# The second block's first norm by tokens: squares on ScalarE, the rows turned earlier, the memory's keys turned inside the queries' strip

## The reference

```python
def rmsnorm_2(x, g):
    xf = x.astype(jnp.float32)
    y = xf * lax.rsqrt(jnp.mean(xf * xf, axis=-1, keepdims=True) + EPS)
    return (y * g.astype(jnp.float32)).astype(x.dtype)

h = rmsnorm_2(x, mix_norm[l])
z = h @ w_in[l]            # pool inputs, queries, keys, values, index queries qi, index key ki, weights wi
...                        # heads normed and rotated, index scores, top 64 keys per query, attention
x = x + jnp.concatenate([y_pool, y_attn], axis=-1) @ w_out[l]
...                        # cross attention to 256 memory tokens, with its own normed keys
...                        # mixture of 32 experts, two per token
```

## Time and profile before

| | |
|---|---|
| median of 3 runs | 822.93 us (822.11 to 824.31) |
| the profiled execution | 823.26 us |
| its span in the profile | 821.5 us |
| mean granted TensorE clock | 0.93 of 2.4 GHz |
| TensorE busy | 735.7 us, 90% of the span |
| VectorE busy | 389.3 us, 47% |
| ScalarE busy | 321.0 us, 39% |
| DMA, mean | 257 GB/s |

### The profile page before, as it was taken

How to read it: one execution, slowest core, us unless ns; L and a number is a source line. 1 busy time by engine, 2 the same in 40 slices (tenths; PEclk the granted TensorE clock), 3 DMA queues, 4 the chain that set the end, 5 groups by cost and what they waited for, 6 DMA issues and landing times.

```text
span 821.5 us, 13037 instructions
## 1 busy us (share of the span) xinstructions
PE 735.7 (90%) x5447; PEld 589.6 (72%) x5448; DVE 389.3 (47%) x761; ACT 321.0 (39%) x596; POOL 21.4 (3%) x54
## 2 busy tenths in 40 slices
PE   6699999999999999999998998686889999879785
PEld 4276687897999999999897776675674666545342
DVE  1446996537554555555627798465341111111011
ACT  2335564626444444445544655555340111011011
POOL 4000001000000002000000000000000000000000
PEclk8699998979999999999977999797789999998899
DMA  9998984419667664337341332085777999999996
GB/s 326 398 410 328 410 322 115 154 53 333 231 206 237 213 209 163 128 132 253 118 154 65 117 139 103 11 356 195 266 295 286 420 420 420 421 419 421 421 415 211
DMA packets 71475, 211.44 MB, mean 257 GB/s; under 512 B 7351, under 2 KB 34133, under 8 KB 55542
## 3 DMA queue, kind: packets, MB, share of 16 engines
q1 hardware_dynamic: 70370, 209.91, 67.2%
q0 software_dynamic: 800, 0.63, 0.6%
q10 hardware_dynamic: 244, 0.03, 0.0%
HBM read 209.51 MB, written 1.05 MB: 256 GB/s over the span
## 4 chain that ended last, share of the span: by engine, by line
PE 66%; DMA 10%; DVE 8%; ACT 5%; SPq 5%; issue 4%; ACTq 0%; DVEq 0%
PE ps L1848 10%; PE ps L1849 9%; PE ps L1850 9%; SPq L403 5%; PE ps L1858 5%; PE ps L1859 5%; PE ps L1860 5%; PE ps L2448 4%; DMA ring<-in_expert_w_up_dram 3%; DMA ring<-in_expert_w_gate_dram 3%; PE ps L1909 3%; DMA ring<-in_ada_w_dram 2%; PE ps L1923 2%; DVE LO L1113 2%; PE ps L2424 2%
## 5 line engine op out<-in xcount | busy, mean ns | idle before, releaser
L1113 DVE TENSOR_TENSOR LO<-ring,HI 128x1024 fp32r<-128x1024 f32 (+1 forms) x135 | 163.7, 1221 | 131.2 <-ACT HI L631 131.2
L631 ACT ACTIVATE HI<-ring 128x1024 fp32r<-128x1024 f32 (+1 forms) x135 | 141.2, 1054 | 136.6 <-PE ps L1850 67.4
L1848 PE MATMUL ps<-AH,HI 128*128 128x256 f32 x320 | 91.0, 284 | 0.1
L1849 PE MATMUL ps<-AL,HI 128*128 128x256 f32 x320 | 90.5, 283 | 0.0
L1850 PE MATMUL ps<-AH,LO 128*128 128x256 f32 x320 | 90.5, 283 | 0.0
L2448 PE MATMUL ps<-ring,ZM 128*32 128x256 f32 x880 | 66.6, 401 | 14.1 <-DMA ring<-in_expert_w_up_dram 11.2
L1848 PE MATMUL ps<-HI,AH 128*128 128x512 f32 (+1 forms) x176 | 69.9, 397 | 7.2 <-DVE AL L1131 6.2
L1849 PE MATMUL ps<-LO,AH 128*128 128x512 f32 (+1 forms) x176 | 68.3, 388 | 0.0
L1850 PE MATMUL ps<-HI,AL 128*128 128x512 f32 (+1 forms) x176 | 68.2, 387 | 0.0
L2448 PEld LDWEIGHTS ps<-ring,ZM 128*32 128x32 f32 x880 | 37.0, 115 | 36.8 <-DMA ring<-in_expert_w_up_dram 15.0
L1848 PEld LDWEIGHTS ps<-AH,HI 128*128 128x128 f32 x320 | 61.4, 192 | 2.8 <-issue 2.5
(11 more groups left out here) (374 smaller groups left out, 1288.9 us busy)
## 6 DMA issues: line engine op xcount, KB each, us to landing
ring<-in_expert_w_gate_dram SPq DMA_DIRECT2D x29, 1024.0 KB, 26.0
ring<-in_expert_w_up_dram SPq DMA_DIRECT2D x26, 1024.0 KB, 23.1
ring<-in_ada_w_dram SPq DMA_DIRECT2D x24, 1024.0 KB, 12.7
ring<-in_expert_w_down_dram SPq DMA_DIRECT2D x23, 1024.0 KB, 25.1
ring<-in_w_ffn_in_dram SPq DMA_DIRECT2D x20, 1024.0 KB, 6.4
ring<-in_w_in_dram SPq DMA_DIRECT2D x17, 1024.0 KB, 5.9
ring<-in_w_ffn_out_dram SPq DMA_DIRECT2D x11, 1024.0 KB, 7.2
ring<-in_w_out_dram SPq DMA_DIRECT2D x8, 1024.0 KB, 7.2
```

The source lines that it names most:

```text
L631: act(HI[:, i % UNITS, 0:w], W.view(name)[:, o:o + w], ACT.Copy).then_inc(s_hi, 1)
L1113: tt(LO[:, i % UNITS, 0:w], W.view(name)[:, o:o + w], HI[:, i % UNITS, 0:w].bitcast(F32), ALU.subtract).then_inc(s_lo, 1)
L1848: mm(dst, lh, rh, start=start, stop=False)
L1849: mm(dst, lh, rl, start=False, stop=False)
```

## The change

The norm's sum of squares is no longer made from XC by TensorE. TensorE turns XC into rows by tokens right behind the strip `qi`, into banks 4 to 7, ahead of `kw`. VectorE makes all four copies to X. ScalarE squares the four half rows with sums, and `mean_rs(0)`, `root_rs(0)`, `recip_rs(0)` give `rs`; the two later norms become the second and third of these helpers' rounds, and the counts of `s_sq` and `s_rs` move with them. The eight squares SQ2 on ScalarE and the matmuls over them are gone. `kw` moves to banks 1 and 3 and waits until ScalarE has read the memory's keys there. The memory's keys are turned behind the third of the queries' four units, and the copies to KM move behind: on ScalarE behind Z of `kw` and one more high half, on VectorE behind the sums of the rotated index queries. ScalarE and VectorE split the units of `q` at new places in their lists. No DMA is added, removed or moved. On GpSimd only a count changes: it waits for 12 and not 8 of `s_sq`, which is the same event.

The diff, without constants, counts of semaphores of the later norms and one view:

```diff
 WOB = (0, 1, 4, 5)
-XTB = (4, 1, 3, 5)
+XTB = (4, 5, 6, 7)
 SCB = ((4, 5), (6, 7))
...
 
-                src = X2[:, t, :].rearrange("q (k p) -> q k p", k=8)[:, :, 64 * n:64 * n + 64] if c else X[:, t, 512 * n:512 * n + 512]
+                src = X2[:, t, :].rearrange("q (k p) -> q k p", k=8)[:, :, 64 * n:64 * n + 64] if c == 8 else X[:, t, 512 * n:512 * n + 512]
                 summed(src, ss[:, t, n:n + 1], s_sq, c + i + 1)
 
             def root_rs(i):
-                ac.wait_ge(s_rs, 4 * i + 3)
+                ac.wait_ge(s_rs, 4 * i + 2)
                 act(rs[:, :], rs[:, :], ACT.Sqrt).then_inc(s_rs, 1)
...
                     bias=colm[:, 3, k:k + 1]).then_inc(s_ah, 1)
-                ac.wait_ge(s_xf, k + 1)
-                act(SQ2[:, k, :], XC[:, k, :], ACT.Square).then_inc(s_sqs, 1)
                 if k in (3, 5):
...
                 act(KS[:, t, :], ps[(1, 3)[t]][:, :], ACT.Copy).then_inc(s_ks, 1)
+            hi_to(S.first["q0"])
+            hi_to(S.first["q0"] + 1)
             ac.wait_ge(s_kn, 1)
             act(mst[:, 8:16], mst[:, 8:16], ACT.Sqrt).then_inc(s_kn, 1)
+
+            for i in range(4):
+                ac.wait_ge(s_xt, i + 1)
+                squares(0, i, i // 2, i % 2)
+            root_rs(0)
 
...
 
-            for i in range(4):
-                hi_to(S.first["qi0"] + i + 3)
-            rooted(rs[:, :], ps[5][:, 0:2], SUM_MIX)
-            ac.wait_ge(s_rs, 1)
+            hi_to(S.first["q0"] + 2)
+            ac.wait_ge(s_rs, 4)
             z_out("qi1", 2048, 512, (0, 2), "qi")
-            hi_to(S.first["kw"] + 3)
             for t in range(NT):
                 if t == 0:
                     ac.wait_ge(s_t0, T0["kw"])
                 else:
                     ac.wait_ge(s_un, S.end["kw"])
-                act(Z[:, t, 2560:NZ], ps[6 + t][:, 0:NZ - 2560], ACT.Copy, scale=rs[:, t:t + 1]).then_inc(s_z, 1)
-
-            for i in (1, 3):
-                ac.wait_ge(s_xp, 4 + i + 1)
-                act(X[:, i // 2, 512 * (i % 2):512 * (i % 2) + 512], ps[XTB[i]][:, :], ACT.Copy).then_inc(s_xt, 1)
-            ac.wait_ge(s_hdp, 1)
-            act(KM[:, 0:2, :], ps[6][:, :].rearrange("p (h n) -> p h n", h=2), ACT.Copy, scale=C1[:, XQK + 1:XQK + 2]).then_inc(s_hda, 1)
+                act(Z[:, t, 2560:NZ], ps[(1, 3)[t]][:, 0:NZ - 2560], ACT.Copy, scale=rs[:, t:t + 1]).then_inc(s_z, 1)
+            hi_to(S.first["q0"] + 3)
 
...
 
-            hi_to(S.first["q0"] + 3)
+            ac.wait_ge(s_hdp, 1)
+            act(KM[:, 0:2, :], ps[6][:, :].rearrange("p (h n) -> p h n", h=2), ACT.Copy, scale=C1[:, XQK + 1:XQK + 2]).then_inc(s_hda, 1)
             hi_to(S.first["q0"] + 4)
...
                 tt(rs[:, :], ss[:, :, 0], ss[:, :, 1], ALU.add).then_inc(s_rs, 1)
-                ve.wait_ge(s_rs, 4 * i + 2)
+                ve.wait_ge(s_rs, 4 * i + 1)
                 ts(rs[:, :], rs[:, :], 1.0 / D, EPS, ALU.mult, ALU.add).then_inc(s_rs, 1)
 
             def recip_rs(i):
-                ve.wait_ge(s_rs, 4 * i + 4)
+                ve.wait_ge(s_rs, 4 * i + 3)
                 ve.reciprocal(rs[:, :], rs[:, :]).then_inc(s_rs, 1)
...
 
+            for i in range(4):
+                ve.wait_ge(s_xp, 4 + i + 1)
+                copy(X[:, i // 2, 512 * (i % 2):512 * (i % 2) + 512], ps[XTB[i]][:, :]).then_inc(s_xt, 1)
+
             ve.wait_ge(s_ks, 10)
             ts(mst[:, 8:16], mst[:, 8:16], 1.0 / P, EPS, ALU.mult, ALU.add).then_inc(s_kn, 1)
-            for i in range(4):
-                lo_to(S.first["qi0"] + i + 3)
+            lo_to(S.first["q0"])
+            lo_to(S.first["q0"] + 1)
             ve.wait_ge(s_kn, 2)
             ve.reciprocal(mst[:, 8:16], mst[:, 8:16]).then_inc(s_kn, 1)
-            ve.wait_ge(s_rn, SUM_MIX)
-            ve.reciprocal(rs[:, :], rs[:, :]).then_inc(s_rs, 1)
-            lo_to(S.first["kw"] + 3)
+            mean_rs(0)
             ve.wait_ge(s_kn, 3)
             for t in range(NT):
                 k3 = KS[:, t, :].rearrange("p (h d) -> p h d", h=4)
                 tt(k3, k3, bc(mst[:, 8 + 4 * t:12 + 4 * t], 2, [P, 4, P]), ALU.mult).then_inc(s_kn, 1)
-
-            for i in (0, 2):
-                ve.wait_ge(s_xp, 4 + i + 1)
-                copy(X[:, i // 2, 512 * (i % 2):512 * (i % 2) + 512], ps[XTB[i]][:, :]).then_inc(s_xt, 1)
-            ve.wait_ge(s_hdp, 2)
-            ts(KM[:, 2:4, :], ps[7][:, :].rearrange("p (h n) -> p h n", h=2), C1[:, XQK + 1:XQK + 2], None, ALU.mult).then_inc(s_hdv, 1)
+            recip_rs(0)
+            lo_to(S.first["q0"] + 2)
 
...
             head_sum(2048, 8, 4, s_hqi)
+            ve.wait_ge(s_hdp, 2)
+            ts(KM[:, 2:4, :], ps[7][:, :].rearrange("p (h n) -> p h n", h=2), C1[:, XQK + 1:XQK + 2], None, ALU.mult).then_inc(s_hdv, 1)
             lo_to(S.first["q0"] + 5)
...
             strip(("qi0", "qi1"), (0, 2), OP_MIX, 0, per=2)
-            u, w72 = S.first["kw"], NZ - 2560
-            te.wait_ge(s_lo, u + 1)
-            for t in range(NT):
-                for k in range(8):
-                    hi, lo = parts(u, slice(w72 * k, w72 * k + w72))
-                    ins = exact(ps[6 + t][:, 0:w72], AH[:, k, P * t:P * t + P], AL[:, k, P * t:P * t + P], hi, lo, k == 0, k == 7)
-                ins.then_inc(s_t0 if t == 0 else s_un, 1)
-            for k in range(8):
-                te.wait_ge(s_sqs, SQ_M + k + 1)
-                added_up(5, SQ2[:, k, :], k, 8)
-            te.wait_ge(s_ks, 10)
             for i in range(4):
-                if i == 3:
-                    te.wait_ge(s_rn, SUM_MIX)
                 for k in range(4 * (i % 2), 4 * (i % 2) + 4):
                     ins = tr(ps[XTB[i]][:, P * (k % 4):P * (k % 4) + P], XC[:, k, P * (i // 2):P * (i // 2) + P], ident[:, :])
                 ins.then_inc(s_xp, 1)
-            te.wait_ge(s_z, 4)
+            u, w72 = S.first["kw"], NZ - 2560
+            te.wait_ge(s_lo, u + 1)
+            te.wait_ge(s_ks, 10)
+            for t in range(NT):
+                for k in range(8):
+                    hi, lo = parts(u, slice(w72 * k, w72 * k + w72))
+                    ins = exact(ps[(1, 3)[t]][:, 0:w72], AH[:, k, P * t:P * t + P], AL[:, k, P * t:P * t + P], hi, lo, k == 0, k == 7)
+                ins.then_inc(s_t0 if t == 0 else s_un, 1)
 
...
 
-            te.wait_ge(s_kn, 5)
+            def between_queries(i):
+
+                if i == 2:
+                    te.wait_ge(s_kn, 5)
+                    heads_turned(KS, (6, 7))
+
             te.wait_ge(s_xt, 4)
-            heads_turned(KS, (6, 7))
-            strip(("q0", "q1"), (4, 5), OP_MIX, 0, per=2)
-            te.wait_ge(s_z, 2)
+            strip(("q0", "q1"), (4, 5), OP_MIX, 0, None, between_queries, per=2)
+            te.wait_ge(s_z, 4)
             strip(("k0", "k1"), (0, 1), OP_MIX, 0, per=2)
```

More of the change, by code:

```diff
@@ L120 @@
 RT_AS, RT_NEG = 13, 16
-SQ_X, SQ_A, SQ_G, SQ_B, SQ_U, SQ_F, SQ_M = 0, 4, 6, 8, 10, 18, 26
+SQ_X, SQ_A, SQ_G, SQ_B, SQ_U, SQ_F = 0, 4, 6, 8, 10, 18
 RB_X, RB_A, RB_B, RB_FF, RB_F = 1, 2, 3, 4, 5
-SUM_X, SUM_A, SUM_G, SUM_B, SUM_FF, SUM_F, SUM_MIX = 1, 2, 3, 4, 5, 6, 7
+SUM_X, SUM_A, SUM_G, SUM_B, SUM_FF, SUM_F = 1, 2, 3, 4, 5, 6
 B0, N1, BU, BV, BG, NM, CB, XQK = 0, 16, 24, 28, 32, 36, 44, 48
@@ L222, in build @@
         SQY, GQ = tiles(Zf[:, 0:1024], 4), tiles(Zf[:, 1024:2048], 4)
-        SQ2 = tiles(Zf[:, 3072:5120], 8)
         CV, SG = YT[:, 0:4, :], YT[:, 4:8, :]
@@ L602, in _ @@
                                      bc(hn[:, i, hi:hi + 32], 1, [P, NT, 32]), ALU.mult).then_inc(s_tab, 1)
-            po.wait_ge(s_sq, 8)
+            po.wait_ge(s_sq, 12)
             po.memset(Lp[:, :, 0:4], FILL).then_inc(s_set, 1)
@@ L1003, in added_squares @@
                         squares(c, 2 * n + t, t, n)
-            added_squares(S.first["attn0"], 0, 4)
+            added_squares(S.first["attn0"], 4, 4)
             for kk in range(4):
@@ L1012, in _ @@
                 ins.then_inc(s_ah, 1)
-            root_rs(0)
+            root_rs(1)
             for i in range(4):
                 hi_to(S.first["wq0"] + i + 3)
-            ac.wait_ge(s_rs, 5)
+            ac.wait_ge(s_rs, 8)
             for t in range(NT):
@@ L1044, in _ @@
                 act(AH[:, 2 * kk:2 * kk + 2, :], YT[:, 2 * kk:2 * kk + 2, :], ACT.Copy).then_inc(s_ah, 1)
-            added_squares(S.first["wo0"], 4, 8)
+            added_squares(S.first["wo0"], 8, 8)
             for kk in (1, 3):
@@ L1051, in _ @@
                         scale=gcol[:, k:k + 1]).then_inc(s_moda, 1)
-            root_rs(1)
+            root_rs(2)
             warm(ACT.Exp)
@@ L1635, in _ @@
                 low_out(OP_XQ + kk + 1, kk, 4 + kk, C2[:, NA:NA + 8])
-            mean_rs(0)
-            recip_rs(0)
+            mean_rs(1)
+            recip_rs(1)
             for i in range(4):
@@ L1675, in _ @@
                        ALU.mult).then_inc(s_modv, 1)
-            mean_rs(1)
-            recip_rs(1)
-            ve.wait_ge(s_rs, 9)
+            mean_rs(2)
+            recip_rs(2)
+            ve.wait_ge(s_rs, 12)
```

(18 more changed lines are left out.)

## The result

| | before | after |
|---|---|---|
| median of the runs taken together, us | 825.55 (19 runs, 820.70 to 829.16) | 818.23 (19 runs, 810.88 to 821.98) |
| profiled execution, us (its span) | 823.26 (821.5) | 819.48 (817.6) |
| mean granted clock of it | 0.930 | 0.934 |

The ratio is 0.991, with a 95% interval of 0.9883 to 0.9937: 5.2 to 9.7 us faster. The sign was forecast. The time is 3.9 us above the forecast of 814.3 and 0.4 above the top of the range, 817.8, although the ratio's interval holds the forecast gain of 8.7.

A forecast was written before the change was run, and what follows sets the result against it. TensorE's thin, low-clock stretch from 415.83 to 436.95 us was taken as the bound. 11.4 - 0.87 - 1.8 = 8.7 us gained, from 823.26 to 814.6, or 814.2 by the median; forecast 814.3, range 810.8 to 817.8.

The forecast's parts named there:

- (a): Right behind the index's queries: 16 transposes of X at full clock, 1.74 us, done at 417.57.
- (b): Ahead of `kw`: its wait for ACT to read the keys' banks costs nothing, being ready some 0.5 us early.
- (c): `kw` itself: clock falls at 420.1, so 23 matmuls take 2.54 us and 25 take 5.4, to 425.5.
- (d): Behind `kw`: sums and 3.04 us wait leave TensorE; copies have 6 us cover; first query matmul 11.4 us earlier.
- (f): From late keys to the index's scores: ACT and DVE wait for keys at 435.8; TensorE loses 1.8 us.
- (e): Inside the queries' strip: the keys' 8 transposes now stand there at full clock, adding 0.87 us.
- (g): Ahead of `v`'s fourth low half: DVE's 5.92 us idle time takes up about 3 us of lateness; nothing lost.
- The clock stays up: Rival at `kw`: clock stays up or falls late, gain 10.3 to 12.8, 810 to 812.5 us; chance 0.13.
- The new wait grows: Rival ahead of `v`: clock falls in the longer thin stretch, 1.7 us lost, 816 to 818.5 us; chance 0.2.
- The stream decides: Rival at the end: DMA engines set it from a time the change doesn't move, 823 us; chance 0.03.
- The clock doesn't come back: Rival in the queries' and keys' strips: 1.2 GHz throughout, 17.6 us lost against 8.7, 832 us; chance 0.04.
- The way to the end: Behind the edited stretch: later loads and DMA stream move with TensorE, so one microsecond gained counts as one at the end.

The follow-up runs named there:

- a4: Changed kernel with the 32 one-column sum matmuls back on TensorE behind `kw`, result unused; 824.62 us, ratio 0.9997 to the kernel before.
- a2: Changed kernel with the memory's keys turned behind the first of the queries' units instead of the third; 812.71 us, ratio 0.9856 to the kernel before.
- a3: Changed kernel with the memory's keys turned ahead of the queries' strip, as before the change; 816.11 us, ratio 0.9887 to the kernel before.
- b3: Changed kernel with two unused 512-column matmuls in the wait ahead of the pooling strip; 820.14 us, ratio 0.9945 to the kernel before.
- c2: Changed kernel with two unused 512-column matmuls between the `v` and `u` strips; 818.44 us, ratio 0.9938 to the kernel before.
- b4: Changed kernel with `kw` and half of the rows' turning between the queries' wide matmuls, keys right behind; 811.51 us, ratio 0.9852 to the kernel before.
- filler: Two unused matmuls in the wait ahead of pooling, added to the changed kernel (820.14 us) and to the kernel with spread order (811.85 us).
- doses: Changed kernel with one, two or three unused matmuls of 0.86 us each between the `v` and `u` strips; 818.57, 818.44 and 819.65 us.

## Why the prediction came out as it did

**What bounds the kernel** was read rightly: the stretch from 415.8 to 436.95 held the gain, and a4 shows that by giving it back.

**(a), (b)**: 16 transposes in 1.67 us (1.74 forecast), no wait ahead of `kw`. Right.

**(c)** was off in its size. 23 matmuls of `kw` were to run at full clock and 25 at half; the fall came at 423.20, behind 39, 6.1 us behind the last wide matmul where it had been 4.3. `kw` took 6.37 us instead of 7.94. That is the term that the bound put at 38 fast matmuls and a gain of 10.3, and the local gain of the first pair of profiles, 10.05, lies there rather than at 8.7. On the mean of three profiles before and six after it is 9.0. The clock then returned later than I took it: the first query matmuls run at 0.43 us apart until 429.9, 11 of them where 8 were forecast, 0.6 us lost: the clock came back 4.8 us into the wide matmuls, where 3.5 was assumed.

**(d)** was right, and its cover larger than needed: the copies were done at 420.3, 4.8 us ahead of the first query matmul. VectorE copied the rows from 417.79, ScalarE squared them in four pairs of 0.81 us, and the factor was there at 425.2 (timelines of VectorE and ScalarE):

```profile
417.79 2.48 DVE L1394 COPY X<-ps 128x512 f32<-128x512 f32 x4 [2.48 <-PE ps L2221]
...
425.17 0.16 DVE L1122 RECIPROCAL rs<-rs 128x2 f32<-128x2 f32 x1
```

```profile
420.50 0.62 ACT L644 ACTIVATE CN<-X 128x512 f32<-128x512 f32 x1
421.02 0.19 ACT L644 ACTIVATION_READ_ACCUMULATOR CN<-X 128x1 f32 x1
...
425.36 1.27 ACT L892 ACTIVATE Z<-ps,rs 128x512 f32<-128x512 f32 x2
...
436.25 0.69 ACT L917 ACTIVATE KM<-ps,C 128x512 f32<-128x512 f32 x1 [8.27 <-PE ps L2238]
```

The last row is ScalarE's idle time of 8.27 us for the keys, the wait that (f) is about.

**(e), (f)**: the keys at 435.62 (435.8 forecast), 2.34 us ahead of the scores (2.6 forecast), and a2 and a3 bring it back to 1.14 by moving the keys alone. That the place of the keys sets this wait is shown; the chain's single terms were not taken apart. **(g)**: VectorE's idle time of 5.92 us ahead of `v`'s fourth low half became 2.89, and TensorE did not wait there:

```profile
460.21 1.23 DVE L1110 TENSOR_TENSOR LO<-ring,HI 128x1024 fp32r<-128x1024 f32 x1 [2.89 <-ACT HI L630]
```

**The rivals.** *The clock stays up* happened in part (39 matmuls). *The new wait grows* came true in part of the runs: the wait was 2.34 to 2.39 us in all six profiles of kernels that are the same up to `v`; the clock stayed up through the scores in four of them and fell there in two (b3, c2), which cost 1.5 us where the rival had 1.7. In the seven profiles with a wait of about 1.14 it never fell at the scores. *The stream decides* is refuted by every kernel here, b4 above all. *The clock doesn't come back*: it did. Of its signs of being wrong the prediction met one: the span ended 3.9 us earlier while the `v` strip started 8.5 us earlier.

**The step that failed is "The way to the end" with "How the numbers follow".** Two things in it:

- The level. I took three runs with a median of 822.93 as the kernel's time. The 106 runs of the same program have a mean of 824.3, and 819.9 to 829.2 as their ends. From 824.3 the forecast gain would give 815.6, still 2.7 below the mean of the changed kernel. In the comparison that was forecast the level weighs more: its 19 runs of before have a median of 825.55, 2.6 above my base, and the gain was 7.3 where I had 8.7. With the base right, 825.55 - 8.7 = 816.9 would have been in the range.
- "So I count a microsecond here as one at the end." On the mean of many runs 6.0 of 9.0 us arrive. In the changed kernel's profile the wait ahead of the pooling was followed by a low clock that was not there before (1.6 us), and the `v`-to-experts stretch took 155.80 us against 151.72, with 37.5 us of low clock against 34.1; a further fall at 528.8 us cost some 1.5, and one profile of before has it too (532.1). I had priced TensorE's thin places in the edited stretch at their own clock and those behind it at a fixed one. Between 500 and 600 us such places stand in a row (waits of 4.13, 2.17, 1.8 and 2.0 us, 64-column matmuls), and their clock moves from run to run.

It is not that each microsecond is worth less. Against the kernel before, with its three profiles' mean of 62.1 us and the 824.3 us of its runs, what is gained up to `v` and does not arrive at the end is much the same, however large the gain:

| | gained up to `v`, us | gained in the mean, us | missing |
|---|---|---|---|
| sums back (a4) | 2.6 | -0.3 | 2.9 |
| changed kernel | 9.0 | 6.0 | 3.0 |
| keys ahead (a3) | 11.3 | 8.2 | 3.1 |
| keys earlier (a2) | 14.5 | 11.6 | 2.9 |
| spread (b4) | 14.3 | 12.8 | 1.5 |

(Column one rests on one profile each but for the changed kernel, and all rows share the same base.) So what failed is that the rest of the program was taken to cost the same behind the change as before it. In the profiles the difference stands mostly between `v` and the experts: 153.7 us on the mean of three of before, 156.1 on the mean of nine with the changed rows and no filler (doses taken off), 2.3 more with a standard error of 1.3. Another 1.0 (0.7) stands ahead of the index's queries, where TensorE's work is the same: they start at 403.2 us in the three and at 404.3 on the mean of the other eleven.

The range had no term for that: it was made of mechanisms alone. The changed kernel's runs spread over 12.5 us, with a correlation of 0.72 between a run's time and its low clock. The Trainium skill (TensorE: Matmul & The Clock Gate, Part 1) calls the number of matmuls that run at the low clock "run-variable"; the profiles agree, with no slow matmul of `kw` in a2 and 9 in the changed kernel. It also puts the ramp penalty below 1% of a typical kernel's span. Here falls and returns stand all along the span, 104 to 110 us of it are at the low clock, and the runs of one program lie up to 1.1% (before) and 1.5% (changed) apart.

What stays open is why some 3 us are given back. It might be the alignment of the later thin work to the clock's falls, which any shift would draw anew; against it speaks that five kernels with shifts from 2.6 to 14.5 us all lose 1.5 to 3.1. Or it is a systematic loss, such as the pooling fall, which was seen in no profile of before and in 6 of 9 with the changed rows and no filler. The fillers say that taking this single fall away does not help, since a longer one came behind it both times, and the doses are too coarse to say more. With three profiles of before, both remain possible.

## What to carry to other kernels

Sums of squares by one-column matmuls are dear where they meet a low clock (32 took 6.8 us); squares with sums on an idle ScalarE cost TensorE nothing if what they feed isn't wanted soon. When thin TensorE work can't be removed, try laying it between wide matmuls instead of in a row: in both profiles of the spread order the clock stayed up through the stretch, and its runs are 6.8 us below the changed kernel's; how much of that the spreading brings is not shown, since turning the keys earlier alone brought 5.5. And before a forecast of one per cent, read the spread of the kernel's own runs and put it into the range beside the mechanisms.

## What the runs showed that I had not expected

- The clock's fall is not fixed to the work: with the same instructions ahead and in it, `kw` lost its clock behind 39 matmuls in the changed kernel and not at all in the profile of the one whose keys alone had moved.
- A covered wait need not pay. The fillers took the fall behind the pooling's wait away in both kernels (19.1 to 17.5 us in that stretch), and neither mean fell; in both profiles the next low stretch was longer, 23.9 and 27.3 us for 10.2.
- The amount of low clock is not its price. Between `v` and the experts the kernel before spent 34.1 us at 1.2 GHz in two profiles and 44.4 in the third, and took 151.72, 153.99 and 155.54 us: the first two differ by 2.3 us at the same amount, so it matters which work a fall meets.
